# Expert gate and up product as three fp32r products, with the zero rows written in another sweep

## The reference

```python
padded = (counts + MOE_BLOCK - 1) // MOE_BLOCK * MOE_BLOCK      # MOE_BLOCK = 128
xb = h_pad[row_token].reshape(n_blocks, MOE_BLOCK, d)
def one_group(args):
    xg, e = args
    return (jax.nn.silu(xg @ w_gate[e]) * (xg @ w_up[e])) @ w_down[e]
```

## Time and profile before

| what | value |
|---|---|
| runs of the kernel before | 2336.82, 2340.93, 2343.44 us |
| span of the profiled execution | 2336.9 us (first to last instruction; a time of its own is not given for it) |
| PE busy | 2029.1 us, 87% of the span |
| DVE, ACT, POOL busy | 878.8 us, 514.7 us, 264.3 us |
| mean granted TensorE clock | 0.931 of full speed |
| `sweep_gate_a` | about 683 to 1073 us |
| `experts` | about 1605 to 2209 us |

### The profile page before, as it was taken

The page is one execution under the profiler, slowest core; times in us unless marked ns, Lnnn a source line. Parts: engine busy times, 40 slices in busy tenths (PEclk is TensorE's granted clock), DMA queues, the critical chain, the costliest instruction groups (busy, mean ns, idle before and its releaser), DMA issues. The chain is left out here.

```text
span 2336.9 us, 28937 instructions
## 1 busy us (share of the span) xinstructions
PE 2029.1 (87%) x9297; PEld 1447.6 (62%) x9298; DVE 878.8 (38%) x1851; ACT 514.7 (22%) x1114; POOL 264.3 (11%) x406
## 2 busy tenths in 40 slices
PE   6879999999969999995799999962999999999700
PEld 2368888888757888883588888841444444444300
DVE  2246666666622000002345555551111121111188
ACT  1034444444422010012111111110111111111111
POOL 0000000000000000000001001111111111111166
PEclk9989999999959999998899999986999999999855
DMA  9832222222236434425543443315998544879486
GB/s 299 268 118 91 92 92 83 79 80 90 80 111 222 159 122 150 162 90 183 181 144 135 144 152 136 108 44 175 373 344 299 193 168 173 291 263 364 180 310 236
DMA packets 193704, 407.97 MB, mean 175 GB/s; under 512 B 27702, under 2 KB 123446, under 8 KB 188658
## 3 DMA queue, kind: packets, MB, share of 16 engines
q1 hardware_dynamic: 165588, 312.26, 38.8%
q0 software_dynamic: 20880, 69.03, 8.0%
q10 hardware_dynamic: 7200, 26.22, 2.8%
HBM read 296.47 MB, written 110.99 MB: 174 GB/s over the span
## 5 line engine op out<-in xcount | busy, mean ns | idle before, releaser
L1923 PE MATMUL ex<-expert_ring,gathered_T 128*128 x816 | 361.0, 595 | 4.1 <-DVE gathered_T L1870 2.1
L1923 PEld LDWEIGHTS ex<-expert_ring,gathered_T 128*128 128x128 f32 x816 | 151.8, 191 | 177.2 <-issue 177.2
L267 PE MATMUL mix<-w_mix_hi,hT_hi 128*128 128x512 f32 (+3 forms) x544 | 204.5, 376 | 3.8 <-DVE hT_lo L647 2.6
L269 PE MATMUL mix<-w_mix_lo,hT_hi 128*128 128x512 f32 (+3 forms) x544 | 199.0, 366 | 0.0
L268 PE MATMUL mix<-w_mix_hi,hT_lo 128*128 128x512 f32 (+3 forms) x544 | 198.6, 365 | 0.0
L1944 PE MATMUL ex<-expert_ring,hidden_T 128*128 x400 | 179.9, 592 | 0.0
L1874 DVE SCALAR_TENSOR_TENSOR silu_e<-tanh_e,ex 128x256 f32<-128x256 f32 x51 | 21.5, 421 | 352.5 <-ACT tanh_e L1829 352.5
L1125 DVE SCALAR_TENSOR_TENSOR ma_rows<-tanh_rows,ga 128x512 f32<-128x512 f32 (+1 forms) x34 | 21.8, 683 | 325.6 <-issue 163.4
L267 PE MATMUL gb<-w_b_hi,h_parts_b 128*128 128x512 f32 (+1 forms) x272 | 109.3, 402 | 25.9 <-DVE w_b_lo L1391 18.1
L267 PE MATMUL ga<-w_a_hi,h_parts 128*128 128x512 f32 (+1 forms) x272 | 106.9, 393 | 14.9 <-DVE w_a_lo L1115 14.0
L1944 PEld LDWEIGHTS ex<-expert_ring,hidden_T 128*128 128x128 f32 x400 | 72.1, 190 | 71.7 <-issue 71.7
(11 more groups left out here) (297 smaller groups left out, 3337.4 us busy)
## 6 DMA issues: line engine op xcount, KB each, us to landing
expert_ring<-in_w_gate SPq DMA_DIRECT2D x32, 1024.0 KB, 9.2
expert_ring<-in_w_up SPq DMA_DIRECT2D x32, 1024.0 KB, 12.6
expert_ring<-in_w_down SPq DMA_DIRECT2D x32, 1024.0 KB, 14.6
expert_rows<-y_block ACTq DMA_DIRECT2D x50, 512.0 KB, 7.2
w_ada_ring<-in_w_ada SPq DMA_DIRECT2D x24, 1024.0 KB, 10.2
h_parts<-hT_split SPq DMA_DIRECT2D x16, 1024.0 KB, 5.2
mixer_parts<-oT_split SPq DMA_DIRECT2D x32, 512.0 KB, 8.3
h_parts_b<-hT_split SPq DMA_DIRECT2D x16, 1024.0 KB, 4.9
```

The source lines that it names most:

```text
L267: nc_mm(out, left[0], right[0], start=first, stop=False)
L269: return nc_mm(out, left[0], right[1], start=False, stop=last)
L1923: last = nc.tensor.matmul(ps[2 + par][:, :], xT[par][:, k, :], w[:, bass.ds(slot * WC + k * 2 * EH, 2 * EH)], start=(k == 0), stop=(k == K ...
```

## The change

In `experts`, the fp32 gate and up product becomes three fp32r products. For that, ACT copies the gate and up columns of a block's expert (4096 columns, in two halves) from the ring into a high tile, and DVE subtracts to get the low tile, once per block, two blocks ahead of their use. The transposed rows are split in the same way: ACT now copies both halves, and DVE subtracts both. ACT copies both halves of a result. PE now waits on `w_lo`, and the wait on `w_ready` stands in ACT's program, in `weights(b+2)`, which lies behind `turned(b+1)` and ahead of `store(b-1)` and of the next step's `hidden(b)`. The order on SP of `arrived` and the loads stays; one wait ahead of the load of expert 3 and the zero fill go. The zero fill moves to POOL's program in `sweep_gate_a`, as two DMAs of 128 rows behind the two stores of each of 16 tiles; it now fills all rows of blocks 32 to 63.

```diff
@@ sweep_gate_a
+        zero = sb("zero_rows", [P, D])
+            pool.memset(zero[:, :], 0.0).then_inc(zeroed, 1)
+            pool.wait_ge(zeroed, 1)
+            def unused(i):
+                for n in range(2):
+                    pool.dma_start(s["ys"][bass.ds(i * 2 * P + (NE + n) * P, P), :], zero[:, :]).then_inc(filled, 16)
...
                     store(p * 2 + par, par, P)
+                    unused(p * 2 + par)
             store(NT, 0, MS)
+            pool.wait_ge(filled, 16 * 2 * NT)
@@ experts, SP
             arrived(1, 1)
-            sp.wait_ge(x_in[0], 32)
             load_expert(sp, a, w, 3, 3, w_in[3])
...
-            sp.wait_ge(zeroed, 1)
-            total = listed(sp, 3, 0)
...
                     load_expert(sp, a, w, g * RING + slot, slot, w_in[slot])
-                    unused(g * (-RING) + (PAIRS + RING - 1 - slot), total)
@@ experts, ACT
             def turned(b, par):
                 act.wait_ge(x_turned, b + 1)
-                nc.scalar.copy(xT[par][:, 0:4, :], ps[0][:, :].rearrange("p (k m) -> p k m", m=P)).then_inc(xT_a, 1)
+                if not isinstance(b, int) or b > 1:
+                    act.wait_ge(gu, b - 1)
+                for n in range(2):
+                    last = nc.scalar.copy(xT[par][0][:, 4 * n:4 * n + 4, :], ps[n][:, :].rearrange("p (k m) -> p k m", m=P))
+                last.then_inc(xT_hi, 1)
+
+            def weights(b, par):
+                need, slot = listed(act, 1, b), listed(act, 0, b)
+                act.wait_ge(w_ready, need)
+                if not isinstance(b, int) or b > 1:
+                    act.wait_ge(gu, b - 1)
+                for n in range(2):
+                    nc.scalar.copy(wg[par][0][:, n * HG:(n + 1) * HG], w[:, bass.ds(slot * WC + n * HG, HG)]).then_inc(w_hi, 1)
...
-                nc.scalar.copy(y[:, par, 0:512], ps[5][:, :]).then_inc(y_a, 1)
-                act.wait_ge(y_a, b + 1)
-                act.wait_ge(y_d, b + 1)
+                for n in range(2):
+                    last = nc.scalar.copy(y[:, par, n * 512:(n + 1) * 512], ps[5 + n][:, :])
+                last.then_inc(y_out, 1)
+                act.wait_ge(y_out, b + 1)
...
+            weights(0, 0)
             turned(0, 0)
+            weights(1, 1)
             silu(0, 0)
             turned(1, 1)
+            weights(2, 0)
...
             def step(b, par, before):
                 hidden(b - 1, 1 - par)
                 silu(b, par)
                 turned(b + 1, 1 - par)
+                weights(b + 2, par)
                 store(b - 1, 1 - par, before)
@@ experts, DVE
+            def weights(b, par):
+                slot = listed(dve, 0, b)
+                for n in range(2):
+                    at = slice(n * HG, (n + 1) * HG)
+                    dve.wait_ge(w_hi, b * 2 + 1 + n)
+                    nc.vector.tensor_tensor(wg[par][1][:, at], w[:, bass.ds(slot * WC + n * HG, HG)], wg[par][0][:, at].bitcast(F32),
+                                            ALU.subtract).then_inc(w_lo, 1)
...
-            def step(b, par, before):
+            def step(b, par):
                 silu(b, par)
                 turned(b + 1, 1 - par)
-                store(b - 1, 1 - par, before)
+                weights(b + 2, par)
@@ experts, PE
             def gate_up(b, par):
-                need, slot = listed(pe, 1, b), listed(pe, 0, b)
-                pe.wait_ge(w_ready, need)
-                pe.wait_ge(xT_a, b + 1)
-                pe.wait_ge(xT_d, b + 1)
+                pe.wait_ge(w_lo, b * 2 + 2)
+                pe.wait_ge(xT_lo, b + 1)
...
-                    last = nc.tensor.matmul(ps[2 + par][:, :], xT[par][:, k, :], w[:, bass.ds(slot * WC + k * 2 * EH, 2 * EH)],
-                                            start=(k == 0), stop=(k == KD - 1))
+                    at = slice(k * 2 * EH, (k + 1) * 2 * EH)
+                    last = three(nc.tensor, ps[2 + par][:, :], (xT[par][0][:, k, :], xT[par][1][:, k, :]),
+                                 (wg[par][0][:, at], wg[par][1][:, at]), k == 0, k == KD - 1)
```

More of the change, by code:

```diff
@@ L1009, in sweep_gate_a @@
 def sweep_gate_a(nc, a, s):
+    assert MAX_BLOCKS - NE <= 2 * NT + 1
     with ExitStack() as ctx:
@@ L1026, in sweep_gate_a @@
         stored_ma, stored_pb = (sem("ga_st_ma0"), sem("ga_st_ma1")), (sem("ga_st_pb0"), sem("ga_st_pb1"))
+        zeroed, filled = sem("ga_zeroed"), sem("ga_filled")
         passed = sem("ga_waits_passed")
@@ L1723, in experts @@
         WC = EXPERT_COLS
+        GU = KD * 2 * EH
+        HG = GU // 2
         lists = sb("block_lists", [1, 4 * P], I32)
@@ L1727, in experts @@
         xg = sb("gathered", [P, 2, D])
-        xT = [sb(f"gathered_T{n}", [P, KD, P]) for n in range(2)]
+        xT = [[sb(f"gathered_T{n}_{part}", [P, KD, P], F32R) for part in ("hi", "lo")] for n in range(2)]
+        wg = [[sb(f"gate_up{n}_{part}", [P, GU], F32R) for part in ("hi", "lo")] for n in range(2)]
         th = sb("tanh_e", [P, 2, EH])
@@ L1733, in experts @@
         y = sb("y_block", [P, 2, D])
-        zero = sb("unused_rows", [P, 2 * D])
         lists_in = sem("e_lists_in")
@@ L1737, in experts @@
         idx_in, x_in = (sem("e_idx_in0"), sem("e_idx_in1")), (sem("e_x_in0"), sem("e_x_in1"))
-        x_turned, xT_a, xT_d = sem("e_x_turned"), sem("e_xT_act"), sem("e_xT_dve")
+        x_turned, xT_hi, xT_lo = sem("e_x_turned"), sem("e_xT_hi"), sem("e_xT_lo")
+        w_hi, w_lo = sem("e_w_hi"), sem("e_w_lo")
         gu, tanhed, silued, h_ready, h_turned, hT_ready = [sem(f"e_{n}") for n in ("gate_up", "tanh", "silu", "h", "h_turned", "hT")]
-        down, y_a, y_d, stored = sem("e_down"), sem("e_y_act"), sem("e_y_dve"), (sem("e_stored0"), sem("e_stored1"))
-        zeroed, filled = sem("e_zeroed"), sem("e_filled")
+        down, y_out, stored = sem("e_down"), sem("e_y_out"), (sem("e_stored0"), sem("e_stored1"))
         passed = sem("e_waits_passed")
@@ L1771, in _ @@
             sp.wait_ge(lists_in, 32)
[L1773 to L1779, removed]
-            sp.wait_ge(zeroed, 1)
-            assert PAIRS == NE and RING * 2 <= NE
-            total = listed(sp, 3, 0)
             with sp.Fori(1, NE // RING) as g:
@@ L1790, in _ @@
                     load_expert(sp, a, w, g * RING + slot, slot, w_in[slot])
-                    unused(g * (-RING) + (PAIRS + RING - 1 - slot), total)
             for slot in range(RING - 2, RING):
                 arrived(slot, NE // RING)
-            sp.wait_ge(filled, (PAIRS - RING) * 16)
         @block.gpsimd
         def _(pool):
-            pool.memset(zero[:, :], 0.0).then_inc(zeroed, 1)
             pool.wait_ge(lists_in, 32)
@@ L1868, in turned @@
             def turned(b, par):
-                dve.wait_ge(x_turned, b + 1)
-                nc.vector.tensor_copy(xT[par][:, 4:8, :], ps[1][:, :].rearrange("p (k m) -> p k m", m=P)).then_inc(xT_d, 1)
+                dve.wait_ge(xT_hi, b + 1)
+                for n in range(2):
+                    last = nc.vector.tensor_tensor(xT[par][1][:, 4 * n:4 * n + 4, :], ps[n][:, :].rearrange("p (k m) -> p k m", m=P),
+                                                   xT[par][0][:, 4 * n:4 * n + 4, :].bitcast(F32), ALU.subtract)
+                last.then_inc(xT_lo, 1)
+            def weights(b, par):
+                slot = listed(dve, 0, b)
+                for n in range(2):
+                    at = slice(n * HG, (n + 1) * HG)
+                    dve.wait_ge(w_hi, b * 2 + 1 + n)
+                    nc.vector.tensor_tensor(wg[par][1][:, at], w[:, bass.ds(slot * WC + n * HG, HG)], wg[par][0][:, at].bitcast(F32),
+                                            ALU.subtract).then_inc(w_lo, 1)
             def silu(b, par):
@@ L1877, in silu @@
                 nc.vector.tensor_tensor(h[:, par, :], ps[2 + par][:, EH:2 * EH], sg[:, par, :], ALU.mult).then_inc(h_ready, 1)
[L1879 to L1883, removed]
-            def step(b, par, before):
+            def step(b, par):
                 silu(b, par)
                 turned(b + 1, 1 - par)
-                store(b - 1, 1 - par, before)
+                weights(b + 2, par)
+            weights(0, 0)
             turned(0, 0)
+            weights(1, 1)
             silu(0, 0)
             turned(1, 1)
+            weights(2, 0)
             total = listed(dve, 3, 0)
-            step(1, 1, None)
-            step(2, 0, None)
+            step(1, 1)
+            step(2, 0)
             with dve.Fori(1, PAIRS) as p:
                 with dve.If(p * 2 < total):
-                    step(p * 2 + 1, 1, p * 16)
-                    step(p * 2 + 2, 0, p * 16)
+                    step(p * 2 + 1, 1)
+                    step(p * 2 + 2, 0)
         @block.tensor
@@ L1908, in turn @@
                 if not isinstance(b, int) or b > 0:
-                    pe.wait_ge(xT_a, b)
-                    pe.wait_ge(xT_d, b)
+                    pe.wait_ge(xT_lo, b)
                 for k in range(KD):
@@ L1938, in out @@
                 if not isinstance(b, int) or b > 0:
```

(5 more changed lines are left out.)

## The result

The kernel after took 2351.99 us in the median of four runs (2350.38 to 2353.18), the kernel before 2339.41 in four (2336.82 to 2343.44). The ratio is 1.005, with an interval of 1.0035 to 1.0064: slower by half a per cent. I had forecast 2337 us and a small gain; the time lies inside the range and at the upper edge of the forecast's own range, and its sign is that of the side that I had given 36%.

What follows compares the result with a forecast made beforehand. PE was taken to bound both changed stages. 2336.9 - 71 (period) + 47 (stall) + 10 (clock) + 8 (start) + 2 (end) = 2333 us, 2337 us on the scale of the median; range 2298 to 2375, the forecast's own 2324 to 2352.

Steps and rivals of the forecast that it cites:

- the side that I had given 36%: Whole kernel: slower than before, 0.36; faster had 0.41 and the same 0.23.
- I take a drop at 6 of 14, +10: `experts`: PE's clock falls after 6 of 14 stall pauses, 1.7 us each in `out`; +10 us (0 to 24).
- Zero fill ... Nothing: `sweep_gate_a`: the zero fill moved there costs nothing; were DMA full, 43 us.
- The period: `experts`: a block costs PE 9.97 us instead of 11.40; a term of -71 us from D(1) to D(49).
- The stall: One-block experts: PE idles 1.5 us + L behind the chain of SP's issues, casts and `hidden`; 14 places, +47 us.
- L: Length of SP's third load issue in the stall's chain of 11.5 us + L; taken as 2.1 us, bounds 1.4 to 4.4.
- Rival 1: One-block experts: the stall is small, L near its floor and no clock drops; 2312 us, 19%.
- rival 2: One-block experts: no stall, ACT's wait is met in time; 2290 us, 6%.
- Rival 3: One-block experts: slower, L = 4.4, stall 5.9 us, clock falls in every longer pause; 2374 us, 25%.
- Rival 4: `gate_up`: fp32r matmuls cost their record of 0.39 us, so three products cost 9.4 us; 1%.
- Start and end: `experts`: first blocks later by 8 us behind ACT's casts for block 1; last store later by 2 us.
- rival 5: `experts`: DVE's subtractions with two SBUF inputs hold POOL's gathers; half of 80 us, 2377 us, 4%.

Runs made afterwards that it cites:

- kernel 2: The kernel after with the zero fill put back in SP's program of `experts`, two DMAs per pair of blocks: 2363.81 us, ratio 1.0096.
- kernel 5: kernel 4 with gate and up loaded only once `out` has read the expert's down weights, as in the kernel after: 2306.09 us, ratio 0.9855.
- kernel 1: The kernel before with only the zero fill moved to POOL in `sweep_gate_a`: 2339.85 us, ratio 0.9998.
- kernel 8: kernel 4 with the zero fill put back on SP's queue behind each expert's loads: 2289.14 us, ratio 0.9781.
- kernel 4: The kernel after with each expert's loads and arrival signals split, gate and up released early, down as before: 2284.57 us, ratio 0.9752.

## Why the prediction was wrong

**The step that failed** is the one on the clock: "I take a drop at 6 of 14, +10". The clock fell at 9 of 13 pauses, 1.6 to 3.1 us each, 20.5 in all (0.1 at each of the other four). In this trace all eight pauses of 3.0 us or more were followed by it, and of five shorter ones (2.28 to 2.89) only one. I had a pause of 1.73 us without a drop and one of 1.95 with a drop, and then priced 3.6 us pauses as if they lay between the two. They lie above both, and for 6 of 14 I gave no reason. With a drop at each of the 14 places at the 1.7 that I had, the term would have been 24, near the 20.5.

The length of a pause alone doesn't settle it. Here is one `out` of kernel 2 and one of kernel 5:

```profile
2125.10 3.69 PE L1971 MATMUL ex<-expert_ring,hidden_T 128*128 x8 [3.04 <-ACT hidden_T L1850]
```
```profile
2081.97 5.39 PE L1997 MATMUL ex<-expert_ring,hidden_T 128*128 x8 [2.02 <-ACT hidden_T L1875]
```

In all twelve traces together `out` was long (5.1 to 6.8 us) behind each of 18 pauses above 3.3 us and behind 10 of 20 between 1.95 and 3.3. What decides between these isn't shown.

**The second** is "Zero fill ... Nothing". It cost 2.7 us at the end of its stage (kernel 1). I had counted transfers and POOL's queue and not the stage's end. In all, the stages outside `experts` came out 7.3 us longer where I had 0, and the fill's 2.7 are all of it that is shown to be the change's. Of the rest, 2.1 us lie ahead of `sweep_gate_a`, where no kernel differs from another and the twelve traces start it at 682.2 to 684.5; 1.2 lie within it, and 1.4 in `combine`, which takes 127.5 to 130.0 us in the twelve. These I can't separate from the difference of two executions. The clock and the other stages make 10.5 + 7.3 = 17.8 us; the span missed by 17.2, and the other terms (below) come to -0.7.

**The period** was 10.02, not 9.97: +2.4 us. Casts took 1.900 us each and subtractions 2.289 (predicted 1.93 and 2.29), both hidden, as argued.

**The stall** was right in place, links and size. The third issue took 2.05 us in the mean of 13 loads (1.26 to 3.65) where I had L = 2.1; 11.5 + 2.05 and 1.58 for the clock make 15.13, and the 13 distances have a mean of 15.13. Place by place, 11.5 us, the third issue and what `out` took over 3.60 meet the time from one end of `out` to the next to within 0.6 us at all 13. That L came out right was luck. The rule that I had for it (15.7 less the distance of two loads) gives 0.7 at a distance of 15, and I had read two of the 32 third issues of the kernel before, whose median is 3.84 us and whose longest 9.27 (in the kernel after 1.68 and 3.67). Kernel 5, in which L is out of the chain, has 11.6. Rival 1 (a small stall) and rival 2 (none) are excluded. Rival 3 was nearly right about the clock and wrong about L = 4.4: the stall is not larger than forecast. Rival 4 is excluded by the period.

**Start and end** were +8.4 and +1.1 against +8 and +2.

**POOL held by VectorE's subtractions** (rival 5): a gather's issue took 0.98 to 1.01 us before; after, in the view of the tile `gathered` (ns: min, median, max):

```profile
L1807 POOL DMA_INDIRECT gathered<-h_rows,row_tokens x52: 979/1352/2197, 1617.5 to 2193.8; - x52
```

It was held by up to 1.2 us. Of the 52 issues 17 overlap no subtraction of weights, and these took 0.98 to 0.99 us; the other 35 took 0.98 to 2.20. The Trainium skill, "SBUF — State Buffer", "Who interferes with whom", says that a VectorE instruction with two inputs in SBUF contends with a GpSimd instruction that reads SBUF; the trace agrees as far as a longer issue goes. It cost nothing: PE waited for gathered rows once, at the start. The slack of 2.2 us that the prediction had for one hold was enough.

## What to carry to other kernels

A gain on the busy engine is first paid out to the loop that comes next. Follow a signal's way from where it is raised to the engine that waits, and look at what lies behind the wait on that engine; here one late signal ahead of a cast cost 65 of 69 us, the low clock behind it included. And this loop with queue issues in it was opened by an earlier release or fewer issues ahead of the signal, not by a faster engine: the same split product with the loads taken apart is 2.5% faster than before. Read all rows of an issue that lies in a chain, and not two. When a stall is predicted, price the clock behind it by rows of pauses as long as the stall; where rows go both ways, give both levels.

## What was not expected of the hardware

- The time that the third DMA issue holds SP is not a matter of the distance of loads: 1.3 to 3.7 us for loads 12.5 to 16.9 us apart here, and up to 9.27 in the kernel before. In kernel 8 the second issue took 7.21 us while 411 GB/s were moving. What sets it isn't shown.
- The low clock came behind a pause of 2.02 us and not behind one of 3.04.
- 32 stores of 0.5 MB more on POOL's queue, all landed long before, lengthened the end of their stage from 5.50 to 8.22 us, by the same amount in the kernel after, in kernel 1 and in kernel 4.
- A gather's issue on POOL takes up to 2.2 us in place of 1.0 when VectorE subtracts out of SBUF at the same time.
